# Value stages of a two-block float32 model: 12 coupled pairs with 3 plain pieces between them instead of 9 with 4, and where their sums are made

## What is computed

```python
def block(args):
    ht, et, gt = args
    act = jax.nn.gelu(jnp.einsum('td,ted->te', ht, u[et]), approximate=False)
    return jnp.einsum('te,ted->td', gt * act, v[et])
```

## Time and profile before

| | us |
|---|---|
| median of 3 runs | 2190.53 (2190.46 to 2191.38) |
| the profiled execution, its own time | 2193.5 |
| its span, first to last instruction | 2191.8 |
| TensorE matmuls busy | 2177.8 (99%) |
| VectorE busy | 1744.3 (80%) |
| ScalarE busy | 1247.2 (57%) |
| GpSimd busy | 721.0 (33%) |
| mean granted clock | 0.997 |

### The profile page before, as it was taken

How to read it: one execution, slowest core, us unless ns; L and a number is a source line. 1 busy time by engine, 2 the same in 40 slices (tenths; PEclk the granted TensorE clock), 3 DMA queues, 4 the chain that set the end, 5 groups by cost and what they waited for, 6 DMA issues and landing times.

```text
span 2191.8 us, 42527 instructions
## 1 busy us (share of the span) xinstructions
PE 2177.8 (99%) x14176; PEld 1897.2 (87%) x14176; DVE 1744.3 (80%) x3418; ACT 1247.2 (57%) x1935; POOL 721.0 (33%) x737
## 2 busy tenths in 40 slices
PE   9999999999999999999999999999999999999999
PEld 8899888888888888888998888888888888999887
DVE  8676885888889999767678778888889987558895
ACT  6555556555444566566565565554445655566764
POOL 1505887333344100002088853324440001530000
PEclk9899999999999999999999999999999999999999
DMA  5254555555565565453545555555655545544654
GB/s 175 97 187 160 186 188 186 171 173 172 180 211 180 186 213 179 144 193 127 182 165 191 186 179 172 172 169 187 212 179 197 207 164 174 167 141 158 186 189 162
DMA packets 109833, 386.08 MB, mean 176 GB/s; under 512 B 12544, under 2 KB 15008, under 8 KB 109472
## 3 DMA queue, kind: packets, MB, share of 16 engines
q1 hardware_dynamic: 106864, 382.34, 52.5%
q10 hardware_dynamic: 2864, 2.36, 0.3%
HBM read 383.46 MB, written 1.06 MB: 175 GB/s over the span
## 4 chain that ended last, share of the span: by engine, by line
PE 92%; DVE 5%; POOL 1%; ACT 1%; issue 1%; DMA 0%; SPq 0%; ACTq 0%; DVEq 0%; POOLq 0%
PE bank L2577 24%; PE bank L2549 13%; PE bank L2629 5%; PE bank L2631 5%; PE bank L2630 5%; PE bank L2672 3%; PE bank L2673 3%; PE bank L2674 3%; PE bank L2465 3%; PE bank L2453 3%; PE bank L2457 3%; PE bank L3036 3%; PE bank L2819 1%; DVE w_lo L1374 1%; PE bank L2694 1%; PE bank L2693 1%
## 5 line engine op out<-in xcount | busy, mean ns | idle before, releaser
L666 ACT ACTIVATE w_hi<-ring 128x1024 fp32r<-128x1024 f32 x663 | 699.4, 1056 | 433.9 <-PE bank L2631 187.6
L1374 DVE TENSOR_TENSOR w_lo<-ring,w_hi 128x1024 fp32r<-128x1024 f32 x512 | 625.2, 1223 | 154.2 <-ACT w_hi L666 152.8
L2577 PE MATMUL bank<-x_parts,w_hi 128*128 128x512 f32 x2320 | 583.1, 393 | 0.3 <-ACT w_hi L666 0.3
L2577 PEld LDWEIGHTS bank<-x_parts,w_hi 128*128 128x128 f32 x2320 | 416.9, 189 | 75.0 <-issue 0.4
L550 POOL TENSOR_TENSOR w_lo<-ring,w_hi 128x1024 fp32r<-128x1024 f32 x151 | 364.2, 2418 | 268.2 <-DVE x_parts L1359 163.1
L562 POOL COPY quads<-sco 128x32 f16 (+1 forms) x256 | 227.7, 918 | 443.9 <-DVE sco L1866 443.8
L2549 PEld LDWEIGHTS bank<-x_parts,w_lo 128*128 128x128 f32 x2368 | 324.4, 190 | 24.9 <-DVE w_lo L1374 2.7
L2549 PE MATMUL bank<-x_parts,w_lo 128*128 128x256 f32 x2368 | 335.7, 283 | 0.2 <-DVE w_lo L1374 0.2
L2629 PE MATMUL bank<-w_hi,x_parts 128*128 128x512 f32 x512 | 201.7, 394 | 0.0
L2631 PE MATMUL bank<-w_lo,x_parts 128*128 128x512 f32 x512 | 199.6, 390 | 0.0
L2630 PE MATMUL bank<-w_hi,x_parts 128*128 128x512 f32 x512 | 199.1, 389 | 0.0
(11 more groups left out here) (422 smaller groups left out, 3691.9 us busy)
## 6 DMA issues: line engine op xcount, KB each, us to landing
ring<-u_dram SPq DMA_DIRECT2D x256, 512.0 KB, 3.2
ring<-v_dram SPq DMA_DIRECT2D x220, 512.0 KB, 3.2
ring<-up_dram SPq DMA_DIRECT2D x44, 512.0 KB, 3.4
big<-v_dram SPq DMA_DIRECT2D x36, 512.0 KB, 4.5
ring<-wq_dram SPq DMA_DIRECT2D x32, 512.0 KB, 4.1
ring<-sb_in_dram SPq DMA_DIRECT2D x31, 512.0 KB, 3.3
ring<-od_in_dram SPq DMA_DIRECT2D x25, 512.0 KB, 3.3
ring<-down_dram SPq DMA_DIRECT2D x22, 512.0 KB, 3.2
```

The costliest lines, as they stand in the source:

```text
L666: A(w_hi[:, k % RING, :], ring[:, k % RING, :], ACT.Copy).then_inc(g["w_hi_done"], 1)
L1374: V.tensor_tensor(w_lo[:, k % RING, :], ring[:, k % RING, :], w_hi[:, k % RING, :].bitcast(F32), ALU.subtract).then_inc(g["lo_dve"], 1)
L2577: mm(dst[:, :], hi[:, rows[c]], x_both[:, c, :], start=(c == 0), stop=False, skip_group_check=True)
```

## The change

In both layers:

- HEAD, COUPLED, BETWEEN, TAIL from 5, 9, 4, 5 to 4, 12, 3, 0: 40 plain pieces and 12 couples in the second half (46 and 9 before), three plain pieces behind the last couple (9 before).
- The three subtractions of weight blocks for couples 0 and 1 (`t13` of 1024 columns, `t2` and `t4` of 512) move into the first half: VectorE's loop of nine rounds is split into five and four, and `early_weight_sums` stands between. Each waits for the one ahead of it. The four sums of activation blocks of 128 columns stay where they were.
- ScalarE's high part of the coupled half's first piece stands ahead of its wait for the last gate.
- The fold stands behind all plain pieces' splits in the queues of ScalarE and VectorE; before, it stood two and three pieces ahead of their end.

```diff
-HEAD, COUPLED, BETWEEN, TAIL = 5, 9, 4, 5
+HEAD, COUPLED, BETWEEN, TAIL = 4, 12, 3, 0
+EARLY_SUMS = ("t13", "t2", "t4", "s1", "s3", "s2", "s4")
+SUMS = ("t13", "s1", "t2", "s3", "s2", "t4", "s4")
...
                     if 0 <= s < COUPLED - 2:
-                        sp.wait_ge(*pair_summed(layer, s, 6))
+                        sp.wait_ge(*sums_done(layer, s, "t4"))
                         sp.wait_ge(*pair_low(layer, 4 * s + 1))
                         load_pair(layer, s + 2)
...
                     highs(first_v + k + 1)
                     v_chunk(k)
+                highs(first_v + HALF + 1)
                 act.wait_ge(g["gated"], 64 * layer + 64)
...
-                    if d == DIRECT - 3:
-                        act.wait_ge(*pair_free(layer, COUPLED - 1))
-                        A(pair_ends[:, 0:CB], bank[0][:, :], ACT.Copy).then_inc(g["pair_high"], 1)
+                act.wait_ge(*pair_free(layer, COUPLED - 1))
+                A(pair_ends[:, 0:CB], bank[0][:, :], ACT.Copy).then_inc(g["pair_high"], 1)
...
+            def early_weight_sums(layer):
+
+                dve.wait_ge(g["pieces_used"], starts[f"v{layer}"] + 32)
+                for s in range(2):
+                    blocks = couple_blocks(s)
+                    dve.wait_ge(*pair_arrived(layer, s))
+                    block_sum(blocks, "t13")
+                    dve.wait_ge(*sums_done(layer, s, "t13"))
+                    block_sum(blocks, "t2")
+                    dve.wait_ge(*sums_done(layer, s, "t2"))
+                    block_sum(blocks, "t4")
+
+            def late_sums(layer, s):
+
+                blocks = couple_blocks(s)
+                dve.wait_ge(g["gated"], 2 * (T // GROUP_T) * (layer + 1))
+                if s >= 2:
+                    dve.wait_ge(*pair_arrived(layer, s))
+                    dve.wait_ge(*pair_free(layer, s - 2))
+                    block_sum(blocks, "t13")
+                block_sum(blocks, "s1")
+                if s >= 2:
+                    dve.wait_ge(*sums_done(layer, s, "t13"))
+                    block_sum(blocks, "t2")
+                dve.wait_ge(*sums_done(layer, s, "s1"))
+                block_sum(blocks, "s3")
+                block_sum(blocks, "s2")
+                if s >= 2:
+                    dve.wait_ge(*sums_done(layer, s, "t2"))
+                    block_sum(blocks, "t4")
+                dve.wait_ge(*sums_done(layer, s, "s2"))
+                block_sum(blocks, "s4")
...
-                with dve.Fori(0, groups // 3 - 1) as i:
-                    six_of_v(6, {0: (1, 2), 2: (3,)}, {1: (4,), 3: (5,), 4: (6,)}, i)
+                def rounds_of_v(first, count):
+
+                    m = 3 * first
+                    with dve.Fori(0, count) as i:
+                        six_of_v(6 + 6 * first, {0: (m + 1, m + 2), 2: (m + 3,)}, {1: (m + 4,), 3: (m + 5,), 4: (m + 6,)}, i)
+
+                rounds_of_v(0, 5)
+                early_weight_sums(layer)
+                rounds_of_v(5, groups // 3 - 1 - 5)
...
                 for d in range(DIRECT):
                     direct(d)
                     if pair_after(d + 3) >= 0:
-                        pair_sums(pair_after(d + 3))
+                        late_sums(layer, pair_after(d + 3))
```

More of the change, by code:

```diff
@@ L362, in pair_low, with sums_done @@
             return g["pair_low"], (4 * COUPLED + 4) * layer + count
-        def pair_summed(layer, s, count):
-            return g["pair_summed"], 7 * (COUPLED * layer + s) + count
+        def sums_done(layer, s, sum_at):
+            place = EARLY_SUMS.index(sum_at) if s < 2 else SUMS.index(sum_at)
+            at = (3 * s + place if place < 3 else 6 + 4 * s + place - 3) if s < 2 else 7 * s + place
+            return g["pair_summed"], 7 * COUPLED * layer + at + 1
         def unit_bank(u):
@@ L1012, in pair_part @@
                     elif part == 1:
-                        act.wait_ge(*pair_summed(layer, s, 6))
+                        act.wait_ge(*sums_done(layer, s, "t4"))
                         dst, src = pair_hi[b][1], pair_sum[s % 3]
                     else:
-                        act.wait_ge(*pair_summed(layer, s, 7))
+                        act.wait_ge(*sums_done(layer, s, "s4"))
                         dst = act_hi[b][:, (part - 2) * 4 * P:(4, 7)[part - 2] * P]
@@ L1755, in top16, with couple_blocks @@
                         settle()
+            def couple_blocks(s):
+                raw, out, row = pair_raw[s % 2], pair_sum[s % 3], couple_row(s) * T
+                b21, b22, b11, b12 = (raw[:, j * CB:(j + 1) * CB] for j in range(4))
+                t13, t1, t2, t4 = b3(out[:, 0:2 * CB], 2), out[:, CB:2 * CB], out[:, 2 * CB:3 * CB], out[:, 3 * CB:4 * CB]
+                b12_twice = b12.rearrange("p (o n) -> p o n", o=1).to_broadcast([P, 2, CB])
+                a11, a21, a12, a22 = (big[:, row + j * P:row + (j + 1) * P] for j in range(4))
+                s2, s1, s4 = (act_sum[s % 2][:, j * P:(j + 1) * P] for j in range(3))
+                return {"t13": (t13, b12_twice, b3(raw[:, CB:3 * CB], 2)), "t2": (t2, b22, t1), "t4": (t4, b21, t2),
+                        "s1": (s1, a21, a22), "s3": (a21, a21, a11), "s2": (s2, s1, a11), "s4": (s4, a12, s2)}
@@ new lines, in block_sum @@
+            def block_sum(blocks, name):
+                V.tensor_tensor(*blocks[name], ALU.add if name == "s1" else ALU.subtract).then_inc(g["pair_summed"], 1)
+            def early_weight_sums(layer):
[8 more added lines that the diff above has]
+                    block_sum(blocks, "t4")
@@ L1952, in direct @@
                     chunk(k0, d, lambda k, i: big[:, direct_row(k) * T:(direct_row(k) + 1) * T])
[L1954 to L1976, removed]
                 def pair_part(s, part):
@@ L1997, in experts @@
                                 pair_part(s, part)
[L1998 to L2006, removed]
+                dve.wait_ge(*pair_high(layer, 4 * COUPLED + 1))
+                step(V.tensor_tensor(e21, bank[2][:, :], e11, ALU.add))
+                settle()
+                step(V.tensor_tensor(e12, bank[1][:, :], e21, ALU.add))
+                settle()
+                step(V.tensor_tensor(e22, bank[3][:, :], e12, ALU.add))
+                step(V.tensor_tensor(e21, bank[3][:, :], e21, ALU.add))
                 settle()
```

## The result

The kernel after takes 2193.48 us (median of 22 runs, 2190.44 to 2200.59), the kernel before 2189.11 beside it on the same chips (22 runs, 2187.23 to 2195.01). The ratio is 1.0022, 95% interval 1.0016 to 1.0028: slower by 4.4 us by the medians, where 1.9 us less was forecast. Both the sign and the range of the prediction were missed.

The account below looks back on a forecast made before the run. It took TensorE, busy 99% of the span, as the bound. Per layer -2.04 - 1.00 + 2.1 = -0.94 us, both layers -1.9, gave 2188.6 us (0.09% less, "same"), range 2184.3 to 2192.

Parts of the forecast that it names:

- part 3: Coupled half, three pieces between couples: VectorE's 12.51 us fits TensorE's 12.92 us group, nothing queued longer behind SyncE's loads; price 0.
- Part 5: Stage's end, fold behind all pieces: additions into banks may start 3.7 us after the last couple; price 0, at worst 0.5.
- rivals A to D: A: the forecast, 2188.6 us, chance 0.58; D: coupled half's starting stall stays or moves, 2190.5 to 2192, chance 0.17.
- Part 1: Coupled half: three more couples, each 0.68 us less than the two plain pieces it replaces; gain 2.04 us a layer.
- Part 2: Start of coupled half: TensorE's stall for VectorE's chunk split goes, 1.00 us a layer; at worst none of it.
- Rival C: Coupled half: VectorE becomes the bound, a group takes 13.91 us; 2203 us in all; chance 0.10.
- Part 4: Middle of first half: six weight sums take VectorE 5.16 us and cost 2.1 us a layer, bounds 1.6 and 2.8.
- Rival B: First half: the early sums are hidden, gains stay whole; 2184.4 us, 0.28% faster; chance 0.15.

Follow-up runs that it names:

- The last experiment but one: sums split, with 15 couples, two plain pieces between them and a couple's parts in reversed order: 2364.11 us, 1.0796 against the kernel before.
- tables early: The kernel after, with the second layer's table loads waiting for the last even couple's sums and first low part: 2188.78 us, 1.0004 against before.
- before, tables late: The kernel before, with only the table loads' wait moved to three pieces ahead of the stage's end: 2192.54 us, 1.0020 against before.
- sums split: tables early, with couple 0's three early weight sums ahead of the sixth round and couple 1's two rounds later: 2184.05 us, 0.9979 against before.

## Why the prediction was wrong, and where it was right

**What failed: the paragraph on SyncE in part 3.** It said that nothing is queued longer behind SyncE's loads, at price 0. It had looked at the loads inside the stage only. The change moves the last couple from nine pieces ahead of the stage's end to three, and `pair_free(1, COUPLED - 1)` is also what the tables' loads wait for, with the next stage's weights behind them. Part 5 noted that three pieces follow now instead of nine and asked what that does to ScalarE's copy and VectorE's fold; the same question was not put to SyncE's queue. Price: 3.3 us of stall and 0.8 behind it at the lower clock level, 4.1 in all, against the 1.9 that were to be won. Two kernels show it: after without the wait, and before with it (2.9 and 0.8 us). With the wait taken out, the median of 2188.78 lies in the forecast's range. None of the rivals A to D had this cause in it.

**It is in the second layer alone**, and the prediction worked out one layer and doubled it. What follows the stage is another program there. That shortcut hid it.

**Part 1, right.** A couple in place of two pieces is 0.68 us less, and coupled halves of 166.09 us stand against the 166.1 of the forecast.

**Part 2, right in its result.** The stall of the earlier trace rows is gone, both in after and without the early high part; and 1.85 us of stall come when the early weight sums go. So it is the sums' move that removes it, and the high part, to which the walk gave the 1.2 us from 746.95 to 748.15, does nothing for it.

**Part 3, VectorE, right.** The walk gave it 12.51 us a group. The timeline of after, VectorE, the starts of three couples' sums:

```profile
771.41 1.21 DVE L1774 TENSOR_TENSOR sco<-big 128x1024 f32<-128x1024 f32 x1
...
783.92 1.21 DVE L1774 TENSOR_TENSOR big<-big 128x1024 f32<-128x1024 f32 x1
...
796.42 1.21 DVE L1774 TENSOR_TENSOR big<-big 128x1024 f32<-128x1024 f32 x1
...
821.70 1.23 DVE L1774 TENSOR_TENSOR big<-big 128x1024 f32<-128x1024 f32 x1 [0.19 <-PE bank L2728]
```

Two groups of 12.51 and 12.50 us, and from 821.70 it waits for TensorE by 0.19: it is ahead, not behind. Rival C did not come. The last experiment but one shows that its mechanism exists all the same, one piece further on, and as a wait rather than as work: a group there took 17.1 us where VectorE's work was 11.04.

**Part 4, right in after.** The forecast was 2.1 us a layer; measured were 2.00 and 1.94, and 2.47 and 2.24 with the tables early, still inside the bounds of 1.6 and 2.8. The first stall, at 678.50, is 1.18 us (1.35 forecast). Six sums took 5.27 us to the start of the next instruction, where 5.16 had been taken from rows. By the Trainium skill ("VectorE: DVE Perf Modes", "The DRAIN you can't avoid") a semaphore between VectorE instructions costs nothing extra, which with the rows' steps would make 4.70; this trace does not agree. Rival B, hidden sums, fell for the block of six; it holds for two blocks of three.

**Part 5, right.** In layer 0 the last couple ends at 912.0 (ScalarE's copy of bank 0 starts at 912.04) and the additions into the banks at 915.51: 3.5 us behind it, 3.7 in the walk. TensorE doesn't wait for them: the coupled half of 166.09 has no stall.

**The sum again, from the runs.** -6.1 for the coupled halves, +3.9 for the first halves, +3.3 for the stall at the end, +3.5 behind it and +0.4 ahead of the first value stage are the 5.1 us between the profiled executions; the medians differ by 4.4. Where the 3.5 behind the stage arise is seen by the time at which the same matmul starts, counted from the stage's end:

| us behind the stage's end, in before | after later by | tables early | before, tables late | sums split |
|---|---|---|---|---|
| 5.5 | 0.8 | 0.0 | 0.8 | 0.0 |
| 24 | 0.8 | 0.0 | 0.8 | 0.0 |
| 30 | 1.9 | 0.8 | 0.8 | 1.1 |
| 50 | 2.6 | 0.8 | 0.8 | 1.9 |
| 215 | 2.6 | 0.8 | 0.8 | 1.9 |
| 279 | 3.5 | 1.6 | 0.8 | 1.9 |

The first 0.8 arise in the first 5 us, at the lower clock level (next section but one); they come with the stall and go with it. The next 1.1 come with ScalarE's wait for its own transfer (1.66 us in after, at 1865.83, instead of 0.55). For the 0.7 between 30 and 50 us and the 0.9 between 215 and 279 us no cause is shown. So the wait explains 4.1 of the 7.0 us between the forecast and the profiled executions, and most of the rest lies behind the stage, where the prediction had no term either.

## What to carry to other kernels

When a change moves the end of some work inside a stage, list everything that waits for that end, in every queue and in what follows the stage, and what stands behind each wait in its queue: here 1 MB of tables waited for the wrong event, and the next stage's weights stood behind them. A stage that occurs twice is to be worked out twice if what follows it differs. Extra work on an engine with slack in every round is free in portions as large as the lead that it holds over its consumer, and costs the surplus when it comes in one block.

## What was not expected of the hardware

After the 3.3 us in which TensorE was idle at the end of the stage, its granted clock fell to the lower of its two levels (1.2 of 2.4 GHz). The table of stretches of after: ahead of the idle time, in it, behind it, and further on (the last three columns are the granted clock, the DMA share and GB/s).

```profile
1830.00:1835.40 5.40, 5.40 (x26) 4.45 (x24) 3.68 (x6) 0.12 (x1) 0.00 (x0) 1.00 1.01 340
1835.40:1839.10 3.70, 0.36 (x2) 0.00 (x0) 2.45 (x2) 3.50 (x6) 0.00 (x0) 0.94 0.44 136
1839.10:1842.30 3.20, 3.19 (x17) 3.20 (x17) 1.72 (x3) 1.69 (x5) 0.00 (x0) 0.54 0.82 284
1842.30:1846.00 3.70, 3.70 (x33) 3.70 (x32) 3.70 (x9) 3.70 (x9) 1.96 (x6) 1.00 0.06 20
```

The 3.20 us behind it run at 0.54, by which 0.46 x 3.20 = 1.5 us might be lost. The trace shows less. Behind the stage's transposes stand products of the next stage (`w_lo`, L2382 of before, L2415 of after). The first of them starts at 1842.84 in before, at 1845.20 in after, and at 1840.39 in before with its tables late. That is 5.30, 6.10 and 6.05 us behind the stage's end, so 0.8 us are lost at the lower level, and the stall of 3.3 us costs 4.1. With the tables late TensorE had been idle for 2.95 us, and 2.86 us behind that ran at 0.50. With two pieces between couples, each stall of 4.63 us is followed by 4.8 us at 0.50, with matmuls 0.43 apart instead of 0.23:

```profile
810.30:815.10 4.80, 4.79 (x11) 3.77 (x12) 4.07 (x5) 0.18 (x1) 0.00 (x0) 0.50 0.56 178
```

Stalls of 1.2 to 1.6 us, as behind the early sums, left the clock at 1.00.

The clock also fell where TensorE had hardly been idle. In the profiled executions of before, of after and of two pieces between it was at the lower level from about 91 to 104 us, long before the value stages. The stretches of before, and the same two of sums split:

```profile
85.00:91.00 6.00, 5.72 (x38) 4.83 (x38) 5.49 (x13) 1.23 (x1) 4.42 (x5) 0.97 0.24 87
91.00:104.30 13.30, 13.30 (x39) 10.56 (x40) 1.42 (x4) 4.45 (x6) 0.00 (x0) 0.50 0.01 1
```

```profile
85.00:91.00 6.00, 5.79 (x41) 5.05 (x40) 5.75 (x14) 1.75 (x2) 4.80 (x6) 1.00 0.29 91
91.00:104.30 13.30, 11.95 (x56) 9.08 (x57) 4.24 (x8) 9.38 (x15) 0.00 (x0) 1.00 0.00 1
```

The first value stage then starts at 561.5 to 562.2 us in those three, at 557.35 in tables early (3.4 us at the lower level), and at 555.3 to 556.0 in the other five. Before with its tables late, whose program is that of before up to there, starts it at 555.38 where before does at 561.50. So single executions differ by 6 us for a reason that is not in the change, more than the effect that was measured; why it falls in one and not in another no run here shows. Lengths of stretches, as used above, are free of it, and whole spans are not.
